# FFN matmuls that alternate between two PSUM banks, in a transformer stack on one core

## The reference

```python
def swiglu(x, w_in, w_out):
    gate, up = jnp.split(x @ w_in, 2, axis=-1)
    return (jax.nn.silu(gate) * up) @ w_out
```

## Time and profile before

| | |
|---|---|
| median of 3 runs | 1628.66 us (1626.01 to 1629.92) |
| span of the profiled execution | 1629.3 us |
| TensorE busy | 1497.1 us, 92% |
| VectorE, ScalarE, GpSimd busy | 43%, 34%, 34% |
| mean granted TensorE clock | 0.951 |
| DMA | 223.24 MB, mean 137 GB/s |

### The profile page before, as it was taken

One profiled execution on the slowest core, in us unless ns is written; L12 is line 12 of the kernel. 1 busy time (PEld: TensorE's weight loads), 2 busy tenths in 40 slices (PEclk: granted clock), 3 DMA queues, 4 the chain that ended last, 5 costly groups with the idle time before them and its releaser, 6 DMA issues.

```text
span 1629.3 us, 21249 instructions
## 1 busy us (share of the span) xinstructions
PE 1497.1 (92%) x8792; PEld 1284.3 (79%) x8792; DVE 704.1 (43%) x885; ACT 550.6 (34%) x671; POOL 549.9 (34%) x209
## 2 busy tenths in 40 slices
PE   5999989999989999979979997999998888899996
PEld 4999978898668999668878855899967364899985
DVE  1545531353136454231564113566642171456654
ACT  3443310213124544321335111444342163444443
POOL 4655500031135554301021022546521044356541
PEclk9999989899999999989999768999999899999998
DMA  8555557332435555423400022455543402355540
GB/s 285 194 191 190 180 120 224 100 129 78 136 130 169 185 180 182 154 81 111 139 23 1 1 81 93 163 187 191 188 153 117 141 27 88 125 193 188 180 155 26
DMA packets 158212, 223.24 MB, mean 137 GB/s; under 512 B 5452, under 2 KB 135717, under 8 KB 158021
## 3 DMA queue, kind: packets, MB, share of 16 engines
q1 hardware_dynamic: 154284, 216.96, 40.4%
q10 hardware_dynamic: 3864, 5.38, 1.6%
HBM read 219.57 MB, written 2.62 MB: 136 GB/s over the span
## 4 chain that ended last, share of the span: by engine, by line
PE 85%; DVE 6%; ACT 4%; POOL 2%; issue 2%; DMA 0%; DVEq 0%; SPq 0%; POOLq 0%; ACTq 0%
PE ps L734 29%; PE ps L764 14%; PE ps L725 12%; PE ps L827 5%; PE ps L973 3%; PE ps L808 2%; PE ps L797 2%; PE ps L1098 1%; PE ps L958 1%; PE ps L1206 1%; PE ps L1222 1%; PE ps L890 1%; ACT weights_first_parts L1339 1%; PE ps L1093 1%; PE ps L1234 1%
## 5 line engine op out<-in xcount | busy, mean ns | idle before, releaser
L1689 POOL TENSOR_TENSOR weights_second_parts<-weight_bays,weights_first_parts 128x2048 fp32r<-128x2048 f32 x88 | 418.6, 4761 | 407.5 <-ACT weights_first_parts L1339 407.5
L1339 ACT ACTIVATE weights_first_parts<-weight_bays 128x2048 fp32r<-128x2048 f32 x132 | 249.8, 1909 | 174.9 <-PE ps L734 74.5
L734 PE MATMUL ps<-x_first_part,weights_first_parts 128*128 128x256 f32 x1408 | 199.0, 284 | 15.8 <-ACT x_first_part L1320 7.4
L725 PE MATMUL ps<-xT,weight_bays 128*128 128x256 f32 (+1 forms) x896 | 201.3, 386 | 2.6 <-DVE xT L1837 2.6
L734 PEld LDWEIGHTS ps<-x_first_part,weights_first_parts 128*128 128x128 f32 x1408 | 184.8, 192 | 21.2 <-issue 15.9
L734 PE MATMUL ps<-x_second_part,weights_first_parts 128*128 128x256 f32 x1408 | 201.3, 287 | 0.0
L734 PE MATMUL ps<-x_first_part,weights_second_parts 128*128 128x256 f32 x1408 | 198.5, 285 | 0.0
L725 PEld LDWEIGHTS ps<-xT,weight_bays 128*128 128x128 f32 (+1 forms) x896 | 171.5, 193 | 29.4 <-DVE xT L1837 3.3
L734 PEld LDWEIGHTS ps<-x_second_part,weights_first_parts 128*128 128x128 f32 x1408 | 184.9, 195 | 0.0
L734 PEld LDWEIGHTS ps<-x_first_part,weights_second_parts 128*128 128x128 f32 x1408 | 182.4, 193 | 0.0
L1863 DVE TENSOR_TENSOR hidden_second_part<-arena,hidden_first_part 128x512 fp32r<-128x512 f32 x44 | 117.9, 2679 | 42.4 <-ACT hidden_first_part L1329 42.4
(11 more groups left out here) (343 smaller groups left out, 1818.7 us busy)
## 6 DMA issues: line engine op xcount, KB each, us to landing
weight_bays<-in_w_ffn_in SPq DMA_DIRECT2D x44, 1024.0 KB, 5.1
weight_bays<-in_ffn_w_in SPq DMA_DIRECT2D x44, 1024.0 KB, 5.1
weight_bays<-in_w_ffn_out SPq DMA_DIRECT2D x22, 1024.0 KB, 4.9
weight_bays<-in_ffn_w_out SPq DMA_DIRECT2D x22, 1024.0 KB, 4.9
weight_bays<-in_w_in SPq DMA_DIRECT2D x19, 1024.0 KB, 5.4
weight_bays<-in_hyb_w_in SPq DMA_DIRECT2D x13, 1024.0 KB, 5.2
weight_bays<-in_ple_w_gate SPq DMA_DIRECT2D x8, 1024.0 KB, 4.9
weight_bays<-in_w_out SPq DMA_DIRECT2D x4, 1024.0 KB, 4.8
```

What stands on the lines that cost most here:

```text
L725: mm = nc.tensor.matmul(dst, lhs(k), xT[:, k] if rhs is None else rhs(k), start=(k == 0), stop=(k == n - 1), **kw)
L734: mm = nc.tensor.matmul(dst, w[:, k, j * P:(j + 1) * P], x[:, k], start=(n + k == 0), stop=(n == 2 and k == KD - 1))
L1339: nc.scalar.activation(hi, raw, ACT.Copy).then_inc(*w_hi_ready.inc(f, g, kind, of - g))
L1689: nc.gpsimd.tensor_tensor(lo, raw, hi, ALU.subtract).then_inc(*w_lo_g.inc(f, g, kind, of - g))
```

## The change

In the first projection the feature tile j becomes the innermost loop: `split_features` takes both tiles' destinations and issues, for each part and slice, one matmul for tile 0 and one for tile 1, so that consecutive matmuls write into two banks in turn and read the same moving operand. In the second projection the half becomes the innermost loop: consecutive matmuls share the stationary operand and write into two banks in turn. Since both of banks 4 and 5 are now written from the second matmul of a stage, `norm` waits for the second signal of `x_second_part` and not the first, in the four FFNs and the three gated projections.

```diff
                 if n in SPLIT:
-                    pe.wait_ge(*x_lo_d.at(n, 0))
+                    pe.wait_ge(*x_lo_d.at(n, 1))
...
-            def split_features(dst, hi, lo, j, first=None):
+            def split_features(dst, hi, lo, first=None):
 
                 for n, (w, x) in enumerate(((hi, x_hi), (lo, x_hi), (hi, x_lo))):
                     if n == 2 and first:
                         pe.wait_ge(*x_lo_d.at(first, 3))
                     for k in range(KD):
-                        mm = nc.tensor.matmul(dst, w[:, k, j * P:(j + 1) * P], x[:, k], start=(n + k == 0), stop=(n == 2 and k == KD - 1))
+                        for j in range(2):
+                            mm = nc.tensor.matmul(dst[j], w[:, k, j * P:(j + 1) * P], x[:, k], start=(n + k == 0), stop=(n == 2 and k == KD - 1))
                 return mm
...
-                        for j in range(2):
-                            mm = split_features(ps[:, 4 + 2 * (g % 2) + j, n * SEQ:(n + 1) * SEQ], *parts[("gate", "up")[n]], j,
-                                                f if g == 0 and n + j == 0 else None)
+                        dst = [ps[:, 4 + 2 * (g % 2) + j, n * SEQ:(n + 1) * SEQ] for j in range(2)]
+                        mm = split_features(dst, *parts[("gate", "up")[n]], f if g == 0 and n == 0 else None)
                         through(mm, key, i)
...
                     for t in range(TT):
-                        for half in range(2):
-                            for n, (x, w) in enumerate(((hid_hi, hi), (hid_lo, hi), (hid_hi, lo))):
-                                for j in range(2):
+                        for n, (x, w) in enumerate(((hid_hi, hi), (hid_lo, hi), (hid_hi, lo))):
+                            for j in range(2):
+                                for half in range(2):
                                     mm = nc.tensor.matmul(bank(2 * t + half), x[:, g % 2, j, t * P:(t + 1) * P],
                                                           w[:, j, half * 512:(half + 1) * 512],
                                                           start=(g == 0 and n + j == 0), stop=(g == GROUPS - 1 and n == 2 and j == 1))
```

## The result

The changed kernel takes 1638.08 us in the median of 7 runs (1634.86 to 1641.19), against 1628.66 us for the kernel before (1625.97 to 1635.3, 7 runs on the same chip). The ratio is 1.0053, with a 95% interval of 1.0034 to 1.0073: slower, by more than 0.3%. The profiled execution took 1634.86 us with a span of 1633.1 us, so 1.8 us lie around the span, and not nothing, as was taken for the kernel before; it is the quickest of the seven.

A forecast was written before the change was run, and what follows sets the result against it. TensorE was taken as the bound, its matmuls end to end at full clock. Zero from both projections and gated projections plus 2.85 us of FFN waits on 1628.66 gave 1631.5 us, range 1606 to 1645.

The forecast's parts named there:

- Rivals 1 and 2: Writes into one bank hold the array up, 56 us less, chance 0.10; only second projection gains, 4 to 15.7 us, chance 0.12.
- The argument from the blocks that already ended with a bank switch: First projection: blocks of 8 with a bank switch take 0.96 us, those without 0.95, so alternation gains 0 ns per matmul.
- neither the half of the weight tile nor the repeat of x should matter: First projection: tile 0's and tile 1's blocks take alike, so the order of operands was taken as 0 ns per matmul.
- rival 3: Matmuls of both projections: the new order makes reads collide more, 14.7 us more, 1646 us; chance 0.11.
- The wait, 0.8 us for each FFN start: Start of each FFN: waiting for VectorE's second x_second_part signal delays the first matmul 0.8 us; three FFNs pay it fully.
- If the clock rises at the same moment as before: First FFN's start: with less time at half rate, the wait costs 0.45 us there, sum 2.85 us; otherwise 3.2 us.
- Rival 4: FFN starts and gated projections: longer idle time drops the clock once more, 1.2 us per FFN plus 2.4 us, 1639; chance 0.13.
- Rival 5: FFN time: cycling banks makes the clock fall, a tenth at half clock, 35 us more, 1666 us; chance 0.03.

The follow-up runs named there:

- kernel before kept busy: Kernel before plus float32 matmuls nobody reads, 10 ahead of the transposes and 5 behind them, ahead of ffn2, conv0, conv1: ratio 0.996.

## Why the prediction was right or wrong

**Nothing from the banks: right, and shown.** The steady group reads as forecast, and alternating banks in the old order gives 11.41 and 5.54 us to the last digit. Rivals 1 and 2 fall. The argument from the blocks that already ended with a bank switch was sound. The rest over pure streaming, 12 and 17 ns for each matmul, stays unexplained; it isn't the bank.

**The order of operands: 0 taken, 1.6 us in the steady groups.** The step said that neither the half of the weight tile nor the repeat of x should matter. It doesn't in steady state; I had not read a group's first two blocks, which are quicker in the old order. This has a tenth of rival 3's price; that reads collide, as the rival has it, is not shown. At the level of the kernel the 1.6 us are not resolved.

**The wait, 0.8 us for each FFN start: right in size.** 0.78 us in the trace, 2.9 ± 0.7 us in the kernel with the wait alone at equal clock, against 2.85, and 2.8 us in the four FFN stages of its profile. In the first FFN the quick part did begin at the same moment as before, the condition that was set, and 0.30 us of the wait are left where 0.45 was forecast. Free in the gated projections: right, 0.24 us of idle time left where about 0.2 was forecast.

**The step that fell short is the sum, "1628.66 + 2.85 = 1631.5 us": it has no term for the clock.** "If the clock rises at the same moment as before" was weighed for the first FFN only; what a shift of everything behind it does to the clock of the whole kernel was put at nothing in the forecast, without a row that says so. Over its 19 runs the changed kernel is 1637.57 us in the mean, 6.05 above the 1631.52 of before (72 runs; the median of 1628.66 that the sum starts from came from three). 2.9 us of that are there at equal clock; the mean clock of 0.948 against 0.951, at 10.9 us for each 0.01, makes the other 3.1. The forecast of no measurable change was wrong. That the time lies in the range is no merit of the account: the range was made wide for the rivals.

**Rival 4 came near in number, and its mechanism didn't happen where it put it.** It gave 1639 us at a chance of 0.13, as one more half-clock stretch of 1.2 us at each of the four FFN starts, behind the longer idle time, and 2.4 us in the gated projections. Neither is found in the runs. The gated projections absorb the wait (-0.1 ± 0.7 us), and behind 2.67 us of idle time instead of 1.79 group 0 of the second FFN takes 13.13 us instead of 13.18, and those of the two later ones no more than before either. At the first FFN an extra loss in some runs isn't excluded. What is shown is that the clock part comes with the wait ahead of the FFNs, in 19 runs of the changed kernel, 12 of the wait alone and 6 of the wait in FFNs only, and goes when the wait is early (mean clock 0.950). That idle time ahead of an FFN can lower the clock there is shown too, but at other lengths than this change has: 1.05 us (in the kernel before kept busy) against 1.79 and 1.83, and 4.10 against 1.79.

**Rival 5, a clock that falls because of the cycling, did not happen.** The mean clock with both projections alternating and the early wait is 0.950, that of before 0.951, and in the changed kernel TensorE is busy without a pause from 90.50 to 203.00 us at a granted clock of 1.00, as before. The Trainium skill's warning in "TensorE: Matmul & The Clock Gate", section "A second HAM failure mode: psum-queue depth-cycling", is not borne out by this kernel.

**What stays open.** Why a later start of the FFNs lowers the mean clock. The profiles lose it in stages that the change doesn't touch: the latent attention's first projection, the hybrid mixer, the mixer between the first two FFNs. But the profile with both alternating and the early wait has some of these longer forms too, so that they can't be put down to the wait one by one. Why the wait in the FFNs alone always came out at 0.943, below the wait everywhere, wasn't tried further.

## What to carry to other kernels

Where TensorE already runs its matmuls end to end at the full clock, look in the trace for a place where the planned alternation already happens once, and compare the intervals there: here it answered the question ahead of the run. What costs is what the edit needs besides, here a wait one signal later. Price a wait at the start of a dense matmul phase not only by its length but also by the clock, and look for the loss in the whole kernel: here about half of the wait's cost went with a lower mean clock, and at three of the four places of the wait nothing of that half was found. Compare kernels at equal mean clock before explaining a few microseconds. Here, filling the idle time ahead of three FFNs with matmuls that nobody reads was worth more (0.4%) than the change that was tried, and it gives the fastest version of this study.

## What was not expected of the hardware

The granted clock differed where the idle time between the last added matmul and the FFN was 1.05 against 1.83 us, with the same instructions around it but for the order of the FFN's own matmuls: 1.00 against 0.91 over the 18 to 19 us of the stage's beginning, in each of three FFNs. From 1.79 to 2.95 us of idle time ahead of the later FFNs nothing more was lost there. Matmuls of 256 columns of fp32r have two steady intervals, 118 and 120 ns, by which tile is loaded, and they are some nanoseconds shorter for the first 16 matmuls behind 512-column ones, 8 in 0.93 to 0.94 us against 0.95 to 0.96, only in the order in which one tile's slices follow one another.
